# Dilated attention: eight equal steps a pass in place of four pairs

## The chip, the cores and the metric

One core of a Trainium2 chip runs the whole program. The metric is the device time of one execution in microseconds (us), median of several runs. The engines are TensorE (PE, whose weight loads are listed apart as PEld), VectorE (DVE), ScalarE (ACT), GpSimd (POOL) and SyncE (SP). They run their own instruction streams and meet by semaphores.

## What is computed

Two transformer-like blocks on one sequence of 1024 rows by 1024 features, all in float32. The change touches one stage of the second block, attention in three dilations:

```python
DILATED_GROUPS = ((128, 1), (512, 4), (2048, 16))
for g, (window, dilation) in enumerate(DILATED_GROUPS):
    q = partial_rope(qkv[:, :, 0, g], positions)
    k = partial_rope(qkv[:, :, 1, g], positions)
    o, lse = dilated_attention(q, k, qkv[:, :, 2, g], window, dilation)
    outs.append(o)
    lses.append(lse)
alpha = jax.nn.softmax(jnp.stack(lses, axis=0), axis=0)
attn = jnp.sum(alpha[..., None].astype(x.dtype) * jnp.stack(outs, axis=0), axis=0)
```

Inside a dilation the rows are split into residue classes, and each block of 128 queries sees its own and the previous 128 keys of its class (band mask, softmax, product with the values). There are 8 heads of 64. `qkv` is a product of the normed input with columns of `w_in`. A later stage (spatial gating) needs other columns of the same product.

## The kernel before

**Passes.** The stage `Dilated` works in 12 passes. Pass `i` is one pair of heads in one of the dilations (1, 4 and 8 in turn, the last standing for 16 with a mask). A pass has 8 blocks `b` of 128 queries. While a pass does its attention, TensorE fills in the projection of later passes: four feature tiles of queries and keys for pass i+1 and two of values for pass i+2, each of 24 matmuls of 512 columns (line 319, called feature passes below; 8 of high halves first, then 16 with low halves), so 144 feature passes in a pass. In pass 11 and the end of pass 10 nothing is left to project, and 16 gate tiles (line 274, 24 matmuls of 256 columns each) for the stage behind stand there.

**A block** on TensorE is a turn (line 2896: 2 or 4 transposes of the probabilities `PB` into bank 6), the values (line 2908: 2 or 4 program instructions, twice as many rows in the trace, into bank 7) and the scores of the block two further on (line 2879: 2 program instructions, 4 in the trace, of 128 or 256 columns). Blocks with a previous block of their class have the larger form. Between them: DVE adds the mask and takes the row maximum (`top`, line 2778), ACT takes the exponentials (`exps`, line 2651) and copies the turned probabilities out of bank 6 (`take_turned`, line 2661), DVE copies the output rows out of bank 7 (`rows`, line 2785), and POOL stores them (line 2714).

**Around it.** DVE rotates each query or key tile: `rotate` (lines 2747 and 2749) reads the bank, `rotate_end` (lines 2757 and 2761) writes `QR` or `KR`. A bank that held tile n is free for tile n+2 when tile n is rotated, so `qk` and `v` wait for `rotated`; gate tiles 0 and 1 wait for the last two rotations. `turn_v` (line 2861, 4 transposes, two of them a pass) turns the values of the next pass into bank 6, ACT copies them out (`v_rows`, line 2638). One pass in three from pass 5 has `turn_pair` twice (line 2542, 4 transposes of the combined rows into bank 6, copied out by `pair_features`, line 2548). Each weight unit is loaded by SP, split by ACT into a high half (`split_hi`, line 258) and by POOL into a low half (`split_lo`, line 266).

**Order.** It is written out by hand for each engine. A pass is four quarters of two blocks. TensorE does in each: half a tile (12 feature passes), turn b, scores b+2, half a tile, values b, turn b+1, half a tile, values b+1, scores b+3, and behind them a `turn_v` (quarters 0 and 1) or a `turn_pair` (quarters 2 and 3). ACT, DVE and POOL follow the same quarters. On POOL the split of a unit stands behind the store of block 0:

```python
                    store(i, 0)
                    if i + 2 < self.N:
                        split_lo(e, self.v_unit(i + 2), KT * P)
                    else:
                        split_lo(e, unit_no(self.u + 2 * self.N + i - 10))
```

Of the kernel before, what the change touches and what calls it, by code (L numbers as in the profile page):

```python
# [86 lines left out]
def hybrid_kernel(nc, A, out):  # L87
    ctx = ExitStack()
    with ctx:
# [217 lines left out]
        def tile_part(pe, u, m, half, bank, n, ready, begins, part):  # L307
# [4 lines left out]
            lo, hi = {None: (0, 24), 0: (0, 12), 1: (12, 24)}[part]  # L312
# [2108 lines left out]
        class Dilated(Stage):  # L2421
# [44 lines left out]
            def gate_tile(self, i, j):  # L2466

                return 12 * (i - 10) + j - 8 if i == 11 or (i == 10 and j >= 8) else -1
# [140 lines left out]
            def act(self, e):  # L2609
# [7 lines left out]
                def gate_tile(i, j):  # L2617
                    s = self.gate_tile(i, j)
                    if s >= 0:
# [54 lines left out]
                for i in range(self.N):  # L2674
                    qk, v = i + 1 < self.N, i + 2 < self.N
                    for q in range(4):
                        b = 2 * q
                        if q == 3 and v:
                            features(i + 2, 0)
                        gate_tile(i, 3 * q)  # L2680
                        take_turned(i, b)
                        exps(i, b + 2)
                        if q == 3 and self.pair_at(i, 0) is not None:

                            self.load_pair(e, self.pair_at(i, 0))
                        if q == 2 and self.pair_at(i, 1) is not None:
                            self.pair_exps(e, self.pair_at(i, 1))
                        gate_tile(i, 3 * q + 1)
                        take_turned(i, b + 1)
                        gate_tile(i, 3 * q + 2)  # L2690
                        exps(i, b + 3)
                        if q == 0:
# [4 lines left out]
                        if q == 2 and v:  # L2697
                            split_qk(i + 2)
                        if q == 2 and not qk:
                            split_hi(e, unit_no(self.u + 2 * self.N + 2))  # L2700
                        if q < 2 and qk:
                            v_rows(i + 1, q)
                        if q >= 2 and self.pair_at(i, 2) is not None:
                            self.pair_features(e, self.pair_at(i, 2), q - 2, 6)
                        if q == 3 and v:
# [31 lines left out]
            def dve(self, e):  # L2737
# [55 lines left out]
                for i in range(self.N):  # L2793
                    more = i + 1 < self.N
                    for q in range(4):
                        b = 2 * q
                        if q == 1 and more:
                            rotate(i + 1, 1)
                        top(i, b + 2)
                        if q == 1 and more:  # L2800
                            rotate_end(i + 1, 1)
                        if q % 2 == 0 and more:
                            rotate(i + 1, (0, 0, 3)[q])
                        rows(i, b)
                        if q % 2 == 0 and more:
                            rotate_end(i + 1, (0, 0, 3)[q])
                        if q == 1 and more:
                            rotate(i + 1, 2)
                        rows(i, b + 1)
                        top(i, b + 3)  # L2810
                        if q == 1 and more:
                            rotate_end(i + 1, 2)
                        c = self.pair_at(i, 1)
                        if c is not None and q == 1:
                            self.pair_largest(e, c)
                        if c is not None and q == 2:
                            self.pair_shares(e, c)
                            self.pair_weighted(e, c, 0)
                        if c is not None and q == 3:
                            self.pair_second(e, c)  # L2820
                        if q == 0 and self.pair_at(i, 2) is not None:
                            self.pair_third(e, self.pair_at(i, 2))

            def pe(self, e):

                def qk(i, n, part):
                    if part == 0:
# [7 lines left out]
                def v(i, n, part):  # L2835

                    if part == 0:
# [16 lines left out]
                def turn_v(i, n):  # L2854
                    e.wait_ge(v_feat.sem, self.vf + 2 * i + 2)
                    if i:

                        e.wait_ge(p_taken.sem, self.pt + 8 * (i - 1) + 2 * n + 2)
# [23 lines left out]
                def turn_p(i, b):  # L2882
# [3 lines left out]
                    if b in (2, 4) and i + 1 < self.N:  # L2886
# [326 lines left out]
```

## Time and profile before

| | us |
|---|---|
| median of 3 runs (3544.68 to 3549.17) | 3545.74 |
| the profiled execution, its own time | 3545.94 |
| its span in the trace | 3544.1 |
| PE busy, share of the span | 3467.8, 98% |
| the 12 passes, first scores to last values | 1823.0 to 2400.0 |

A row of a timeline gives the start, the duration and the instruction, with `x4` where equal neighbours are merged, and in brackets the engine's idle time before it and who ended it. The ends of matmuls are modelled and overlap the next one, so what a matmul costs on TensorE is read from start to start and not from its duration. The granted clock is given as a share of 2.4 GHz.

### The profile page before, as it was taken

The numbers are of one execution on the slowest core, as the hardware profiler recorded it, in microseconds if no ns is written. First come the engines' busy times: TensorE is split into PE (matmuls) and PEld (weight loads), VectorE is DVE, ScalarE is ACT, GpSimd is POOL, SyncE is SP. The second block draws the span as 40 slices with busy tenths as digits, with TensorE's granted clock in tenths as the row PEclk, the third lists the DMA queues.
The fourth block names the chain that finished last, engine by engine and source line by source line (L and its number), as shares of the span: only waits on it lengthen the run. The fifth ranks groups of instructions, "written<-read, shape, count | busy, mean of one in ns | idle before, by whom it ended". The sixth has DMA issues, their size and how long they took to land.

```text
span 3544.1 us, 44150 instructions
## 1 busy us (share of the span) xinstructions
PE 3467.8 (98%) x17275; PEld 2866.0 (81%) x17275; DVE 1393.4 (39%) x2446; ACT 931.5 (26%) x1568; POOL 959.9 (27%) x415
## 2 busy tenths in 40 slices
PE   7899999999999999999999999999999999999999
PEld 6688877888888888888778878887888888888887
DVE  6873443122445333333653344435123322231224
ACT  4233434222242111111433333333222311111112
POOL 1352102232315333333212222212322232322321
PEclk9999999999999999999999999999999999999999
DMA  4233012212212111111221212213122111111111
GB/s 132 56 80 90 31 54 66 66 48 76 95 65 102 47 47 48 52 53 47 72 87 48 66 47 66 77 36 129 55 71 101 48 54 48 47 47 47 47 47 60
DMA packets 203979, 226.85 MB, mean 64 GB/s; under 512 B 19225, under 2 KB 177605, under 8 KB 203341
## 3 DMA queue, kind: packets, MB, share of 16 engines
q1 hardware_dynamic: 180524, 171.16, 15.8%
q10 hardware_dynamic: 18944, 43.22, 3.5%
q0 software_dynamic: 4384, 10.74, 0.9%
q8 instruction: 85, 1.39, 0.2%
q14 instruction: 42, 0.34, 0.0%
HBM read 191.30 MB, written 31.69 MB: 63 GB/s over the span
## 4 chain that ended last, share of the span: by engine, by line
PE 90%; DVE 5%; ACT 2%; issue 1%; DMA 1%; POOL 0%; SPq 0%; ACTq 0%; DVEq 0%; POOLq 0%
PE ps L274 18%; PE ps L319 16%; PE ps L295 13%; PE ps L302 13%; PE ps L301 13%; PE ps L778 5%; PE ps L2908 2%; PE ps L2879 1%; PE ps L336 1%; PE ps L2391 1%; PE ps L2896 1%; PE ps L510 1%; PE ps L2372 1%; POOL wlo L266 0%; DVE tm L1615 0%
## 5 line engine op out<-in xcount | busy, mean ns | idle before, releaser
L266 POOL TENSOR_TENSOR wlo<-raw,whi 128x2048 fp32r<-128x2048 f32 (+1 forms) x162 | 700.1, 4322 | 1695.4 <-ACT whi L258 1694.7
L301 PE MATMUL ps<-h_lo,whi 128*128 128x512 f32 x1856 | 722.0, 389 | 0.0
L302 PE MATMUL ps<-h_hi,wlo 128*128 128x512 f32 x1856 | 722.0, 389 | 0.0
L258 ACT ACTIVATE whi<-raw 128x2048 fp32r<-128x2048 f32 (+1 forms) x162 | 288.1, 1778 | 903.0 <-PE ps L295 599.2
L295 PE MATMUL ps<-h_hi,whi 128*128 128x512 f32 x1856 | 459.2, 389 | 2.7 <-issue 2.7
L295 PEld LDWEIGHTS ps<-h_hi,whi 128*128 128x128 f32 x1856 | 347.8, 188 | 75.8 <-issue 3.8
L301 PEld LDWEIGHTS ps<-h_lo,whi 128*128 128x128 f32 x1856 | 348.4, 188 | 72.5
L302 PEld LDWEIGHTS ps<-h_hi,wlo 128*128 128x128 f32 x1856 | 348.3, 188 | 72.3
L1198 DVE TENSOR_TENSOR big<-big,ps 128x512 f32<-128x512 f32 x400 | 274.7, 687 | 241.8 <-PE ps L274 241.5
L319 PE MATMUL ps<-h_lo,whi 128*128 128x512 f32 x880 | 351.5, 399 | 0.1
L319 PE MATMUL ps<-h_hi,wlo 128*128 128x512 f32 x880 | 344.3, 391 | 0.0
L274 PE MATMUL ps<-whi,f_hi 128*128 128x512 f32 x800 | 311.2, 389 | 0.0
L274 PE MATMUL ps<-wlo,f_hi 128*128 128x512 f32 x800 | 311.2, 389 | 0.0
L274 PE MATMUL ps<-whi,f_lo 128*128 128x512 f32 x800 | 311.2, 389 | 0.0
L319 PE MATMUL ps<-h_hi,whi 128*128 128x512 f32 x880 | 230.4, 404 | 6.9 <-DVE cacc L1842 6.6
L1132 POOL TENSOR_TENSOR f_lo<-fv,f_hi 128x512 fp32r<-128x512 f32 x108 | 142.2, 1317 | 316.6 <-DVE f_hi L1189 316.6
L319 PEld LDWEIGHTS ps<-h_lo,whi 128*128 128x128 f32 x880 | 165.2, 188 | 40.9 <-issue 5.7
L319 PEld LDWEIGHTS ps<-h_hi,whi 128*128 128x128 f32 x880 | 159.6, 190 | 45.4 <-DVE cacc L1842 7.0
L319 PEld LDWEIGHTS ps<-h_hi,wlo 128*128 128x128 f32 x880 | 165.4, 188 | 32.6
L1183 DVE TENSOR_TENSOR fv<-fr,ps 128x512 f32<-128x512 f32 x44 | 30.2, 687 | 404.8 <-PE ps L302 404.8
L1072 ACT ACTIVATE fr<-ps 128x512 f32<-128x512 f32 x108 | 64.2, 598 | 447.0 <-PE ps L302 445.3
L274 PEld LDWEIGHTS ps<-whi,f_lo 128*128 128x128 f32 x800 | 150.2, 188 | 31.2
(335 smaller groups left out, 4796.3 us busy)
## 6 DMA issues: line engine op xcount, KB each, us to landing
raw<-in_w_ff_dram SPq DMA_DIRECT2D x32, 1024.0 KB, 5.2
raw<-in_w_in_dram SPq DMA_DIRECT2D x57, 512.0 KB, 4.5
raw<-in_w_in_dram SPq DMA_DIRECT2D x28, 1024.0 KB, 5.4
raw<-in_w_ffn_gate_dram SPq DMA_DIRECT2D x11, 1024.0 KB, 5.4
raw<-in_w_ffn_up_dram SPq DMA_DIRECT2D x11, 1024.0 KB, 5.4
raw<-in_w_ffn_down_dram SPq DMA_DIRECT2D x11, 1024.0 KB, 4.9
yt<-y_keep ACTq DMA_DIRECT2D x16, 512.0 KB, 4.0
raw<-in_w_out_dram SPq DMA_DIRECT2D x8, 1024.0 KB, 5.1
```

The lines of the kernel that those rows point to most:

```text
L258: nc.scalar.activation(whi[c % 2][:, 0:cols], raw[c % 2][:, 0:cols], ACT.Copy).then_inc(s_hi.sem, 1)
L266: nc.gpsimd.tensor_tensor(wlo[c % 2][:, 0:cols], raw[c % 2][:, 0:cols], whi[c % 2][:, 0:cols].bitcast(F32), ALU.subtract).then_inc(s_lo.se ...
L274: last = nc.tensor.matmul(out_, lhs(a, k), rhs(b, k), start=(k == 0 and n == 0), stop=(k == ks - 1 and n == 2))
L295: first = nc.tensor.matmul(ps[:, bank + n, :], w(0, k, m * P, P), src[0][:, k, sl], start=k == 0, stop=False)
L301: nc.tensor.matmul(ps[:, bank + n, :], w(0, k, m * P, P), src[1][:, k, sl], start=False, stop=False)
L302: last = nc.tensor.matmul(ps[:, bank + n, :], w(1, k, m * P, P), src[0][:, k, sl], start=False, stop=k == ks - 1)
L319: x = nc.tensor.matmul(ps[:, bank, :], w(a, k, m * P, P), H[b][:, k, sl], start=j == 0, stop=j == 23)
L778: return nc.tensor.matmul(ps[:, t, :], H[a][:, 4 * (j % 2) + k, t * P:(t + 1) * P], w[j](b, k, 0, HALF), start=start, stop=stop)
L1072: nc.scalar.activation(fr[:, n, :], ps[:, n, :], ACT.Relu if self.g == 1 else ACT.Silu).then_inc(act_a.sem, 1)
L1132: nc.gpsimd.tensor_tensor(f_lo[:, c % 2, m, half * HALF:(half + 1) * HALF], fv[:, n % 2, :], f_hi[:, c % 2, m, half * HALF:(half + 1) * HA ...
L1198: nc.vector.tensor_tensor(dst, dst, ps[:, 4 + t % 4, :], ALU.add).then_inc(dve_b.sem, 1)
L2908: last = nc.tensor.matmul(ps[:, 7, h * HD:(h + 1) * HD], PT2[:, b % 2, h, c, :], V2[:, i % 2, b - 1 + c, h, :], start=c == cs[0], stop=c == 1)
```

## The change

A pass becomes eight equal steps, one for each block. TensorE does in step b: 9 feature passes, what stands between (a `turn_v` in steps 1 and 2, a `turn_pair` in steps 6 and 7), 9 feature passes, turn b, values b-1, scores b+2. A tile is cut wherever a step ends. The values come one step later than their turn, also over the pass's end, and so do `rows` on DVE and the stores on POOL. DVE's rotations stand in steps 1, 2, 3 and 5: `rotate`, then `rows` of the block before, `top`, then `rotate_end`. On ACT `split_hi` of the value unit (or of a gate unit) moves from behind `exps` of block 3 to behind that of block 2, and that of the next query and key unit from the end of the third quarter to the end of step 5. No instruction is added or taken out.

```diff
-                    for q in range(4):
-                        b = 2 * q
-                        half_tile(3 * q)
+                    for b in range(8):
+                        tiles = list(self.gate_tiles(i, b))
+                        passes(18 * b, 18 * b + 9)
+                        for t in tiles[1:]:
+                            gate_tile(t - 1)
+                        between(b)
+                        passes(18 * b + 9, 18 * b + 18)
+                        for t in tiles[-1:]:
+                            gate_tile(t)
                         turn_p(i, b)
+                        if 8 * i + b:
+                            value(*divmod(8 * i + b - 1, 8))
                         score(i, b + 2)
...
+            def gate_tiles(i, b):
+
+                if i == 10:
+                    return {5: (0,), 6: (1,), 7: (2, 3)}.get(b, ())
+                if i == 11:
+                    return range(4 + b // 2 * 3 + b % 2 * 2, 6 + b // 2 * 3 + b % 2)
+                return ()
...
+                    for b in range(8):
+                        n = {1: 0, 2: 1, 3: 2, 5: 3}.get(b) if i + 1 < self.N else None
+                        if n is not None:
+                            rotate(i + 1, n)
+                        if 8 * i + b:
+                            rows(*divmod(8 * i + b - 1, 8))
                         top(i, b + 2)
+                        if n is not None:
+                            rotate_end(i + 1, n)
```

TensorE before, two blocks in the middle of a pass of dilation 8 (`PB` is turned, `PT` the turned probabilities, `KR,QR` the scores):

```order
L2896 MATMUL ps<-cst,PB 128x128 x2
L2879 MATMUL ps<-KR,QR 128x128 x2
L319 MATMUL ps<-h_lo,whi 128x512
...
L2908 MATMUL ps<-V,PT 128x64 x2
L2896 MATMUL ps<-cst,PB 128x128 x2
L319 MATMUL ps<-h_hi,whi 128x512 x8
...
L2908 MATMUL ps<-V,PT 128x64 x2
L2879 MATMUL ps<-KR,QR 128x128 x2
L2861 MATMUL ps<-cst,VF 128x128 x4
```

TensorE of the change, the same place:

```order
L319 MATMUL ps<-h_hi,whi 128x512 x3
L2851 MATMUL ps<-cst,VF 128x128 x4
L319 MATMUL ps<-h_hi,whi 128x512 x5
...
L2884 MATMUL ps<-cst,PB 128x128 x2
L2896 MATMUL ps<-V,PT 128x64 x2
L2869 MATMUL ps<-KR,QR 128x128 x2
L319 MATMUL ps<-h_lo,whi 128x512
```

Three places a pair where feature passes break off have become one a block; no values stand behind a feature pass any more, and each `turn_v` stands between two runs of them.

TensorE of the change in pass 10, steps 5 and 6, with gate tiles 0 and 1 (`ps<-whi,h_hi` to `ps<-whi,h_lo` is one tile):

```order
L319 MATMUL ps<-h_hi,wlo 128x512
L274 MATMUL ps<-whi,h_hi 128x256
...
L274 MATMUL ps<-whi,h_lo 128x256
L2884 MATMUL ps<-cst,PB 128x128 x4
L2896 MATMUL ps<-V,PT 128x64 x2
L2869 MATMUL ps<-KR,QR 128x256 x2
L274 MATMUL ps<-whi,h_hi 128x256
```

DVE of the change at that place, the last rotation of all:

```order
L2746 STREAM_SHUFFLE rp<-ps 128x512
L2748 SCALAR_TENSOR_TENSOR rt<-ps,rope 128x512
L2784 COPY OS<-ps 128x2x64
L2777 ISA PB,OS<-ps,mask_p 128x256
L2777 ISA OS 128x1
L2777 ISA PB,OS<-ps,mask_p 128x256
L2777 ISA OS 128x1
L2756 SCALAR_TENSOR_TENSOR rp<-rp,rope 128x512
L2760 TENSOR_TENSOR KR<-rt,rp 128x8x64
```

Before, `top` of block 7 stood behind the end of this rotation; now it stands ahead of it, and TensorE has nothing between the scores of block 7 and gate tile 1, which waits for the rotation.

## Rows read from the trace of the kernel before

**Rows 1.** The page, part 1: busy time, share of the span, instructions.

```profile
PE 3467.8 (98%) x17275; PEld 2866.0 (81%) x17275; DVE 1393.4 (39%) x2446; ACT 931.5 (26%) x1568; POOL 959.9 (27%) x415
```

**Rows 2.** Waits of PE, 1820 to 2402 us: total, times, longest.

```profile
PE ps L274 <- POOL wlo L266: 4.1, 1, 4.1
PE ps L2896 <- ACT YC L2548: 1.2, 3, 0.4
PE ps L2896 <- ACT V L2638: 0.8, 1, 0.8
```

**Rows 3.** Timeline of PE in pass 4 (dilation 4), one pair of blocks.

```profile
2018.10 0.39 PE L319 MATMUL ps<-h_lo,whi 128*128 128x512 f32 x1
...
2018.78 0.39 PE L319 MATMUL ps<-h_hi,wlo 128*128 128x512 f32 x1
2019.01 0.38 PE L2896 MATMUL ps<-cst,PB 128*128 128x128 f32 x2
2019.32 0.49 PE L2879 MATMUL ps<-KR,QR 64*128 64x128 f32 x4
2019.75 0.50 PE L319 MATMUL ps<-h_lo,whi 128*128 128x512 f32 x1
2020.08 0.39 PE L319 MATMUL ps<-h_hi,wlo 128*128 128x512 f32 x1
...
2022.61 0.56 PE L2908 MATMUL ps<-V,PT 128*128 128x64 f32 x4
2023.00 0.60 PE L2896 MATMUL ps<-cst,PB 128*128 128x128 f32 x4
2023.36 2.10 PE L319 MATMUL ps<-h_hi,whi 128*128 128x512 f32 x8
...
2026.22 1.00 PE L2908 MATMUL ps<-V,PT 128*128 128x64 f32 x8
2027.15 0.70 PE L2879 MATMUL ps<-KR,QR 64*128 64x256 f32 x4
2027.78 0.65 PE L2861 MATMUL ps<-cst,VF 128*128 128x128 f32 x4
2028.19 0.47 PE L319 MATMUL ps<-h_lo,whi 128*128 128x512 f32 x1
2028.51 0.39 PE L319 MATMUL ps<-h_hi,wlo 128*128 128x512 f32 x1
```

**Rows 4.** Timeline of PE in pass 11: gate tiles, an ordinary one and the late one.

```profile
2341.82 0.38 PE L274 MATMUL ps<-whi,h_hi 128*128 128x256 f32 x1
...
2344.79 0.55 PE L2908 MATMUL ps<-V,PT 128*128 128x64 f32 x4
...
2364.21 0.49 PE L2879 MATMUL ps<-KR,QR 64*128 64x128 f32 x4
2368.79 0.58 PE L274 MATMUL ps<-whi,h_hi 128*128 128x256 f32 x1 [4.09 <-POOL wlo L266]
...
2373.82 0.55 PE L2908 MATMUL ps<-V,PT 128*128 128x64 f32 x4
```

**Rows 5.** Stretches: length, busy us of PE, PEld, DVE, ACT, POOL, granted clock, DMA.

```profile
1752.00:1755.00 3.00, 3.00 (x13) 2.61 (x12) 2.93 (x4) 0.65 (x1) 0.00 (x0) 0.54 0.00 0
...
2368.00:2370.00 2.00, 1.21 (x5) 1.21 (x6) 0.00 (x0) 0.00 (x0) 1.25 (x2) 0.50 0.05 10
```

**Rows 6.** Timeline of PE in an earlier stage, around another wait.

```profile
1751.73 1.50 PE L510 MATMUL ps<-cst,xn 128*128 128x128 f32 x8 [2.67 <-DVE xn L491]
```

**Rows 7.** Timelines of PE and DVE, pass 4: scores, a rotation's last step.

```profile
2039.30 0.70 PE L2879 MATMUL ps<-KR,QR 64*128 64x256 f32 x4
...
2041.55 1.21 DVE L2761 TENSOR_TENSOR KR<-rt,rp 128x512 f32<-128x512 f32 x1
```

**Rows 8.** Timeline of POOL, pass 11: a store of rows, and the late low half.

```profile
2345.96 0.54 POOL L2714 DMA_DIRECT2D dil_keep<-OS  x1 [7.25 <-DVE OS L2785]
...
2364.24 4.50 POOL L266 TENSOR_TENSOR wlo<-raw,whi 128x2048 fp32r<-128x2048 f32 x1 [6.00 <-ACT whi L258]
```

More of the change, by code:

```diff
@@ L2464, in take_pairs @@
                 return pair_loaded.take(48 * n), pair_step.take(13 * n), pair_exp.take(n), ct_turned.take(2 * n), ct_taken.take(2 * n)
-            def gate_tile(self, i, j):
-                return 12 * (i - 10) + j - 8 if i == 11 or (i == 10 and j >= 8) else -1
+            @staticmethod
+            def gate_tiles(i, b):
[4 more added lines that the diff above has]
+                return ()
             @staticmethod
@@ L2923, in pe, with passes @@
                 for i in range(self.N):
-                    def half_tile(j):
-                        n, part = j // 2, j % 2
-                        if n < 4 and i + 1 < self.N:
-                            qk(i + 1, n, part)
-                        elif n >= 4 and i + 2 < self.N:
-                            v(i + 2, n - 4, part)
-                        elif self.gate_tile(i, j) >= 0:
-                            gate_tile(self.gate_tile(i, j))
-                    for q in range(4):
-                        b = 2 * q
-                        half_tile(3 * q)
+                    def passes(lo, hi):
+                        for n in range(lo // 24, 6):
+                            part = max(lo - 24 * n, 0), min(hi - 24 * n, 24)
+                            if part[0] >= part[1]:
+                                break
+                            if n < 4 and i + 1 < self.N:
+                                qk(i + 1, n, part)
+                            elif n >= 4 and i + 2 < self.N:
+                                v(i + 2, n - 4, part)
@@ new lines, in between @@
+                    def between(b):
+                        if b in (1, 2) and i + 1 < self.N:
+                            turn_v(i + 1, b - 1)
+                        if b in (6, 7) and self.pair_at(i, 2) is not None:
+                            e.wait_ge(p_taken.sem, self.pt + 8 * i + b)
+                            self.turn_pair(e, self.pair_at(i, 2), b - 6, 6)
+                    for b in range(8):
+                        tiles = list(self.gate_tiles(i, b))
[6 more added lines that the diff above has]
+                            gate_tile(t)
@@ L2936, in pe @@
                         turn_p(i, b)
+                        if 8 * i + b:
+                            value(*divmod(8 * i + b - 1, 8))
                         score(i, b + 2)
-                        half_tile(3 * q + 1)
-                        value(i, b)
-                        turn_p(i, b + 1)
-                        half_tile(3 * q + 2)
-                        value(i, b + 1)
-                        score(i, b + 3)
-                        if q < 2 and i + 1 < self.N:
-                            turn_v(i + 1, q)
@@ L2946, in pe @@
-                        if q >= 2 and self.pair_at(i, 2) is not None:
-                            e.wait_ge(p_taken.sem, self.pt + 8 * i + b + 2)
-                            self.turn_pair(e, self.pair_at(i, 2), q - 2, 6)
+                value(self.N - 1, 7)
         class SpatialGate(Stage):
```

78 lines of the change are left out of this document (27 added, 51 removed).

## The prediction

> **What bounds the kernel now.** I read the page's busy times first: PE is busy for 98% of the span and nobody else for more than 39% [rows 1]. A busy PE may still lose time, since the ends of its matmuls are modelled, so I read the waits of PE in the stage, and then its timeline from start to start. The waits are few: one of 4.1 us for a late low half of a weight unit, three of 1.2 us together for ACT's copy of combined rows, one of 0.8 us for ACT's copy of values [rows 2]. An idle time counts from the end of the last matmul, which is 0.39 us long, where the next usually starts 0.23 us after its start; each wait thus costs 0.16 us more than the view shows: 1.7 us for the three and 0.95 us for the one. All else in the stage's 577 us is instructions at their own pace. So the stage is bound by TensorE's starts, and the change can give or take at three places: the pace where one kind of matmul follows another, the waits that go, and the waits that come.
>
> **The pace at the joints.** A feature pass follows another by 0.68 / 3 = 0.23 us [rows 3]. From the last feature pass of a run to the second of the next run, less two such starts, is what a joint costs. In one pair of blocks of pass 4 [rows 3]:
> - turn (2), scores (128 columns): 2018.78 to 2020.08 is 1.30 us, less 0.46: 0.84.
> - values (4), turn (4): 0.23 to the first, then 0.39, then 0.36, and 0.31 to the second feature pass (the x8 has its second 0.31 in, by the 0.32 of 2028.19 to 2028.51 after transposes of the same kind). 1.29 less 0.46: 0.83.
> - values (8), scores (256), without the `turn_v`: 0.23, 0.93, 0.63, and 0.33 to the second feature pass behind scores (2019.75 to 2020.08). 2.12 less 0.46: 1.66.
>
> Sum 3.33 us a pair. Inside these: a value matmul costs 0.11 (8 against 4 of them differ by 0.54 less the 0.10 by which scores start later behind values than a turn does), but the first behind a feature pass only 0.06 (4 take 0.39, and 4 x 0.11 is 0.44). A transpose costs 0.11, and 0.20 where scores follow it. In the change each block is turn, values, scores between two runs:
> - small turn, large values, scores (128): 0.23 + 0.22 + 0.98 + 0.43 + 0.33 = 2.19, less 0.46: 1.73.
> - large turn, small values, scores (256): 0.23 + 0.44 + 0.54 + 0.63 + 0.33 = 2.17, less 0.46: 1.71.
>
> Sum 3.44, so 0.10 to 0.11 us more a pair. Two things make it: both values of a pair lose the cheap start behind a feature pass (2 x 0.05), and the breaks of the runs, fewer as they are (two in place of three), now all end in the dear return from scores. Over 47 pairs I take 0.10 each: **4.7 us**. The passes of the other dilations have the same joints in other sizes, and the difference is in the joints. The gate tiles break off in the same way.
>
> A `turn_v` stood behind scores and took the dear return on itself: it added 0.41 us from its first transpose to the feature pass (2027.78 to 2028.19) and made the return 0.32 instead of 0.33, so 0.40 us. Between two runs it costs 0.23 + 3 x 0.11 + 0.03 + 0.31 less 0.46, 0.44 us. 22 of them at 0.04 make **0.9 us**. Pace in all: +5.6 us. No row shows values directly behind a turn. The bounds are the cheap start kept (95 x 0.05 us less, so +0.8) and a start as late as that of scores behind a turn (0.09 more for 95, so +14). I take the 0.11 since values and transposes follow each other at 0.11 in the other order (4 values, 0.39 us to the turn), and one kind of fp32 matmul of 128 columns of weights to the next costs that in every row but the two with scores, which use half the rows of the array.
>
> Behind scores the second feature pass starts 0.33 us after the first in place of 0.23, and four values behind a feature pass save 0.05 [rows 3]: at one joint the next weights come late, at the other they come in under the long matmul ahead. The Trainium skill, "TensorE: Matmul & The Clock Gate", section "What happens when you issue a matmul", says that TensorE's queue pulls weight loads ahead of matmuls in flight. If that held at each joint, none would cost anything, before or after, and the sum would be without the 5.6 us; the 0.33 speaks against it, the 0.05 for it.
>
> **Waits that go.** The turn waited three times for the copy of combined rows and once for that of values, because the copies out of bank 6 came late on a busy ACT. In the change nine feature passes stand behind each of them (9 x 0.23 = 2.1 us), ACT has had step b's `exps` by then and copies in 0.6 us. On ACT `split_hi` of 1.9 us stands ahead of the first `pair_features`; it begins some 2.3 us after step 5's scores and ends 4.2 us after them, the copy at 4.8, and the turn that needs it starts 5.3 us after them. So I let these waits go: **-2.65 us**. If the cover is gone they cost what they cost now.
>
> **The late low half.** Gate tile 8 waits for POOL's low half. Before, ACT's `split_hi` behind `exps` of block 3 decided. Now that is a block earlier, and POOL's own queue decides: `store(11, 0)` stands ahead and waits for the rows of block 0, which come a step later. From the values of a block to the store's start 1.17 us pass [rows 4, 8], then 0.54 for its issue and 4.50 for the low half [rows 8]: 6.2 us after the values of block 0. TensorE gets from those values to gate tile 8 by 0.54 (small values to scores), 0.43 (scores) and one gate tile of 2.97 us [rows 4]: 3.9 us. So a wait of 2.3 to 2.5 us stands where 4.58 less 0.43, 4.15 us, stood [rows 4]: **-1.75 us**.
>
> **A new wait.** Gate tile 1 in pass 10 waits for the last rotation. Before, half a tile of other work and two blocks' turns lay between. Now `rotate_end` stands behind `top` of block 7, `top` behind the scores of block 7, and those behind gate tile 0; and TensorE comes from these scores directly to gate tile 1. With scores of 256 columns the last step of a rotation that follows `top` ends at 2041.55 + 1.21 = 2042.76, which is 3.46 us after the scores' start at 2039.30 [rows 7]. TensorE would start the tile 0.63 us after it [rows 3]. **+2.9 us.**
>
> **The end of the stage.** The values of blocks 6 and 7 now follow with nothing between, and the second waits for DVE's copy of the first out of bank 7; the last `turn_pair` also stands right behind a block. From values to the store 1.17 us pass, of which the copy's end is some 0.85 us in, and four values cover 0.44. I take **+0.8 us** for both; 0 if something covers them, 1.5 if both wait for the whole way.
>
> **The clock.** The granted clock fell to 1.2 GHz (0.50) in the late wait of 4.09 us [rows 5], and the gate tile behind it took 2368.79 to 2373.82, 5.03 us, against 2.97 us for an ordinary one [rows 4]: 2.06 us. It also fell after an idle time of 2.67 us in an earlier stage (0.54 granted behind it) [rows 5, 6]. So each of the two waits of 2.9 and 2.4 us may bring it down, or not. I take that one of them does, at 2.0 us, as now: **0**. The bounds are none (-2.0) and both (+2.1).
>
> **Sum.** +5.6 - 2.65 - 1.75 + 2.9 + 0.8 + 0 = +4.9 us. Against the profiled execution's 3545.94 (span 3544.1, 1.8 around it, and 0.2 above the median) that is 3550.8 us. The stage behind starts its own chain with the last rows, so that it moves with them.
>
> **Rivals.**
> - *The joints cost nothing more.* If values behind a turn start as cheaply as behind a feature pass, the pace is +0.8 and the time 3546.1. For it: four values behind a feature pass do save 0.05. Against: the saving needs a long matmul ahead, under which the next weights come in, and a turn's are short. Chance 8%.
> - *The rotation is late in every pass* (slower). Tile 2 starts 12 feature passes into step 2 and needs the rotation that ends in step 1 or so; tile 5 the same in steps 5 and 6. Those twelve end 0.63 + 0.33 + 10 x 0.23 = 3.3 us, and the thirteenth would start 3.5 us, after the scores; the rotation ends after 3.46. There is no slack where scores have 256 columns. It decides from a chain longer than 3.5 us. With 0.3 us more on DVE, 20 such starts cost 6 us: 3556.8. Against: the 3.46 us are measured with both `top`s in them, tile 2 also has a `turn_v` of 0.4 us ahead, and the last step is 0.5 us shorter where the dilation is 1. Chance 12%.
> - *Both new waits bring the clock down* at 2.06 us each: 3552.9, just at the bound of 0.2%. Chance 22%, half of it beyond the bound with the spread of the other terms.
> - *Faster by over 0.2%.* It needs stalls in the old order that starts don't show, or both waits gone and the joints free. Chance 3%.
>
> **How the numbers follow.** A measurement of this kernel can tell about 0.2%, 7.1 us, from no change. The forecast has 55%, with its own range of 3548.5 to 3552.5. Within 0.2% are the forecast, the free joints and half of the case with the clock twice down: 55 + 8 + 11 = 74%. Slower are the late rotations and the other half, 12 + 11 = 23%. Faster 3%. The range of 3546 to 3555.5 takes in the free joints, and both falls of the clock with 2.5 us for the end and the joints; it leaves out most of the late rotations and the gain.
>
> **What would show it.** Right: behind a turn the first values start 0.11 us later, a pair of blocks costs 3.44 us over its feature passes; PE's waits are one of about 2.5 us idle on `rotated` near 2342 us and one of 2.0 us on the low half near 2370; the waits for ACT's copies are gone; a pass is 0.4 to 0.5 us longer. Wrong: waits of feature passes on DVE in each pass, or a pass that is not longer. The forecast falls if the gate tile's wait is covered, or if the clock behaves otherwise than once down.

## The result, and the profile after

| | before | after |
|---|---|---|
| median of four runs, us | 3546.44 (3544.68 to 3549.17) | 3569.75 (3568.49 to 3571.7) |
| ratio, 95% interval | 1 | 1.0064 (1.0049 to 1.0079) |
| profiled execution, us (span) | 3545.94 (3544.1) | 3571.7 (3569.9) |
| stage, first scores to last values, us | 1822.97 to 2400.03: 577.1 | 1825.86 to 2424.69: 598.8 |

The change makes the kernel 23.3 us slower. The forecast was 4.9 us slower, and 3569.75 lies far outside the range of 3546 to 3555.5. Of the 25.8 us between the two spans 21.8 are in the stage. 2.9 lie ahead of it, where the kernel is the same: the first 80 us took 1.1 us more in this execution, the clock fell once more near 150 us (2.6 us) and once less near 1770 us (0.9 us back). 1.1 lie behind the stage.

The page of the changed kernel shows at once that nothing new is bound by throughput. Its first part, which answers [rows 1]:

```profile
PE 3477.1 (97%) x17275; PEld 2871.6 (80%) x17275; DVE 1430.0 (40%) x2446; ACT 935.9 (26%) x1568; POOL 958.6 (27%) x415
```

PE gained 9 us of busy time, and 16 us of idle time came in. DVE grew by 37 us with the same 2446 instructions, and that is the odd number of this page. The waits of PE in the stage (engine, line, waited for: total, times, longest; one more of 0.2 us is in both kernels) answer [rows 2]:

```profile
PE ps L319 <- DVE QR L2760: 15.5, 11, 3.4
PE ps L274 <- DVE KR L2760: 2.7, 1, 2.7
PE ps L274 <- POOL wlo L266: 2.3, 1, 2.3
PE ps L2896 <- DVE OS L2784: 0.5, 1, 0.5
PE ps L2869 <- ACT V L2642: 0.4, 1, 0.4
```

The waits for ACT's copies out of bank 6 are gone, the one for the gate tile and the one for the low half are there, and on top stand eleven waits of feature passes for a rotation, one in each of passes 0 to 10. The prediction had named just this view as the sign that it is wrong. From start to start, the late passes cost 1.2 to 1.5 us each in passes 0 to 9 and 3.6 us in pass 10: 17.4 us.

In pass 4 the timelines of PE, DVE and POOL (start, duration, idle time before, releaser) read:

```profile
2038.99 0.40 PE L319 MATMUL ps<-h_lo,whi 128*128 128x512 f32 x1
2039.22 0.40 PE L319 MATMUL ps<-h_hi,wlo 128*128 128x512 f32 x1
2040.89 1.43 PE L319 MATMUL ps<-h_hi,whi 128*128 128x512 f32 x5 [1.27 <-DVE QR L2760]
```

```profile
2036.35 0.42 DVE L2777 CUSTOM_DVE_ANT_0 PB<-ps,mask_p 128x256 f32<-128x256 f32 x1 [0.44 <-PE ps L2869]
2036.70 0.08 DVE L2777 DVE_READ_ACCUMULATOR2_ANT OS<- 128x1 f32 x1
2036.70 0.42 DVE L2777 CUSTOM_DVE_ANT_0 PB<-ps,mask_p 128x256 f32<-128x256 f32 x1
2037.05 0.08 DVE L2777 DVE_READ_ACCUMULATOR2_ANT OS<- 128x1 f32 x1
2037.05 2.68 DVE L2756 SCALAR_TENSOR_TENSOR rp<-rp,rope 128x512 f32<-128x512 f32 x1
2039.76 1.08 DVE L2760 TENSOR_TENSOR QR<-rt,rp 128x512 f32<-128x512 f32 x1
```

```profile
2036.20 0.54 POOL L2713 DMA_DIRECT2D dil_keep<-OS  x1 [5.51 <-DVE OS L2784]
2036.76 2.41 POOL L266 TENSOR_TENSOR wlo<-raw,whi 128x1024 fp32r<-128x1024 f32 x1
```

One instruction is far too long here: the first step of `rotate_end` takes 2.68 us, where 33 others in the stage take 0.69. It ends at 2039.73, 0.56 us after POOL's subtraction, which runs from 2036.76 to 2039.17. Its two inputs, `rp` and the table `rope`, are both in SBUF, as are POOL's `raw` and `whi`. The two instructions of `top` beside it, which take one input from PSUM, keep their 0.42 us under the same subtraction. In pass 10 the low half is that of a gate unit and takes 4.58 us, and there the step takes 4.84:

```profile
2330.59 4.84 DVE L2756 SCALAR_TENSOR_TENSOR rp<-rp,rope 128x512 f32<-128x512 f32 x1
```

```profile
2330.30 4.58 POOL L266 TENSOR_TENSOR wlo<-raw,whi 128x2048 fp32r<-128x2048 f32 x1
```

Of the 37 us that DVE grew by, 23 are these steps' (25.6 in eleven long ones, less 2.8 in three of the kernel before). Another 13 are three instructions that combine the dilations' rows, with both inputs in SBUF too: two of 128x48 take 4.48 and 4.51 us in place of 0.21, and one of 128x1024 takes 5.84 in place of 1.22, each beside a low half of 4.56. The first, on DVE and then POOL:

```profile
2065.16 4.48 DVE L2520 TENSOR_TENSOR cw<-cw 128x48 f32<-128x48 f32 x1
```

```profile
2065.01 4.56 POOL L266 TENSOR_TENSOR wlo<-raw,whi 128x2048 fp32r<-128x2048 f32 x1 [3.07 <-ACT whi L258]
```

No wait of PE hangs on these three.

What brings the step and the subtraction together is POOL's queue. `split_lo` stands behind `store(i, 0)` in both kernels. Before, the rows of block 0 came in its own step, and the split behind the store still waited 5.4 us for ACT's high half. Now that half is ready some 4 us ahead of the store, the rows come a step later, `rows(i, 0)` stands on DVE just ahead of `top` and `rotate_end`, and the store and the split start behind it, 0.3 us ahead of `rotate_end` (in three passes 0.2 us behind its start).

The kernel before had shown the same thing once, in rows that I did not read. In pass 10 its rotation's step took 3.20 us, under a low half of 4.58:

```profile
2318.60 3.20 DVE L2757 SCALAR_TENSOR_TENSOR rp<-rp,rope 128x512 f32<-128x512 f32 x1
```

```profile
2316.66 4.58 POOL L266 TENSOR_TENSOR wlo<-raw,whi 128x2048 fp32r<-128x2048 f32 x1 [6.30 <-ACT whi L258]
```

It cost nothing there, since no matmul was waiting for that rotation. Two other steps of 0.81 us began 0.26 us before a subtraction ended. And those two subtractions show the reverse: VectorE's addition for the combined rows (128x1024, two inputs in SBUF) ran its usual 1.23 us from 2075.95, and POOL's, which began 0.56 us behind it, took 2.91 us in place of 2.4 (the same at 2218.58 and 2219.14):

```profile
2076.51 2.91 POOL L266 TENSOR_TENSOR wlo<-raw,whi 128x1024 fp32r<-128x1024 f32 x1 [4.21 <-ACT whi L258]
```

The rest of the stage's 21.8 us: the waits that were forecast, their falls of the clock, and the pace. The gate tile and the low half (PE, a gate tile's first matmul behind scores of 256 columns in pass 10, and one behind another gate tile in pass 11):

```profile
2359.70 0.70 PE L2869 MATMUL ps<-KR,QR 64*128 64x256 f32 x4
2363.09 0.39 PE L274 MATMUL ps<-whi,h_hi 128*128 128x256 f32 x1 [2.69 <-DVE KR L2760]
...
2389.19 0.28 PE L274 MATMUL ps<-whi,h_lo 128*128 128x256 f32 x1
2391.78 0.39 PE L274 MATMUL ps<-whi,h_hi 128*128 128x256 f32 x1 [2.31 <-POOL wlo L266]
```

And the stretches at the lower clock (length, busy us of PE, PEld, DVE, ACT, POOL, granted clock, DMA):

```profile
2337.87:2344.70 6.83, 6.83 (x24) 5.57 (x23) 2.63 (x8) 1.26 (x5) 0.56 (x1) 0.50 0.26 87
...
2392.49:2395.90 3.41, 3.41 (x19) 3.41 (x18) 1.55 (x2) 0.00 (x0) 0.00 (x0) 0.50 0.90 294
```

By start-to-start times the stage of before is 568.2 us of pace, 6.8 of waits and 2.1 of the lower clock. The stage of after is 570.8 of pace, 23.6 of waits (17.4 for the rotation, 2.8 for the gate tile, 2.5 for the low half, 0.6 and 0.3 at the end) and 4.5 of the clock. The differences, 2.6 + 16.8 + 2.4, make the 21.8.

### The profile page after: what moved, and what is told of

Read it like the earlier page. It is cut to its first block, busy times and chain, and to the rows that moved or that the text cites. A ratio compares the mean times of both kernels' runs of the same rounds, so it can differ in the third digit from the quotient of the medians.

```text
span 3569.9 us, 44150 instructions
## 1 busy us (share of the span) xinstructions
PE 3477.1 (97%) x17275; PEld 2871.6 (80%) x17275; DVE 1430.0 (40%) x2446; ACT 935.9 (26%) x1568; POOL 958.6 (27%) x415
## 4 chain that ended last, share of the span: by engine, by line
PE 89%; DVE 6%; issue 1%; ACT 1%; DMA 1%; POOL 1%; ACTq 0%; SPq 0%; DVEq 0%; POOLq 0%
PE ps L274 18%; PE ps L319 16%; PE ps L295 13%; PE ps L302 13%; PE ps L301 13%; PE ps L778 5%; PE ps L2896 2%; PE ps L2869 1%; PE ps L336 1%; PE ps L2391 1%; DVE rp L2756 1%; PE ps L2884 1%; PE ps L2372 1%; PE ps L510 1%; POOL wlo L266 0%
## 5 line engine op out<-in xcount | busy, mean ns | idle before, releaser
L295 PE MATMUL ps<-h_hi,whi 128*128 128x512 f32 x1856 | 459.2, 389 | 2.7 <-issue 2.7
L319 PE MATMUL ps<-h_hi,whi 128*128 128x512 f32 x880 | 239.6, 409 | 22.3 <-DVE QR L2760 15.5
L274 PEld LDWEIGHTS ps<-whi,f_hi 128*128 128x128 f32 x800 | 150.2, 188 | 31.2
```

Of the source, the lines that this page charges most:

```text
L274: last = nc.tensor.matmul(out_, lhs(a, k), rhs(b, k), start=(k == 0 and n == 0), stop=(k == ks - 1 and n == 2))
L295: first = nc.tensor.matmul(ps[:, bank + n, :], w(0, k, m * P, P), src[0][:, k, sl], start=k == 0, stop=False)
L319: x = nc.tensor.matmul(ps[:, bank, :], w(a, k, m * P, P), H[b][:, k, sl], start=j == 0, stop=j == 23)
```

## The experiments

Theory A: VectorE's step with two inputs in SBUF is kept out while GpSimd subtracts. Its rival B: the rotation is too slow for its twelve feature passes whatever GpSimd does, as the second rival of the prediction had it. Medians are compared with the kernel before on the same chip, 3545.7 to 3547.1 us.

**The split ahead of the store** takes away what makes them meet, and no work.

```
                 for i in range(self.N):
-                    store(i, 0)
                     if i + 2 < self.N:
                         split_lo(e, self.v_unit(i + 2), KT * P)
...
-                    for b in range(1, 5):
+                    for b in range(5):
                         store(i, b)
```

> The changed kernel with one edit: GpSimd's `split_lo` stands ahead of `store(i, 0)`, not behind it. It then waits only for ScalarE's `split_hi`, which in pass 4 ends at 2032.3 us, and would run from there to about 2034.7 us, clear of the rotation's `rp` step at 2037.05 us. Theory A (the `rp` step is held for as long as GpSimd's subtraction runs): `rp` takes 0.69 us in every pass instead of 2.7 to 3.2 (4.84 in pass 10), the eleven waits of feature tile 2 for rotation 0 go (17.4 us), and with the one of pass 10 its fall of the clock (2.4 us). The low half of the gate units comes earlier too, since its store no longer stands ahead (2.5 us, and perhaps the clock's 2.1). From 3569.8 that gives 3545.5 to 3550 us. Theory B (the chain of the rotation is too long for the twelve feature passes whatever GpSimd does): the chain and its waits of 1.2 to 1.4 us a pass stay, 3562 to 3568 us.

Measured: 3546.38 us, a ratio of 0.9999 (0.9989 to 1.0009) to the kernel before. The eleven waits are gone. DVE and then POOL in pass 4:

```profile
2029.58 0.69 DVE L2755 SCALAR_TENSOR_TENSOR rp<-rp,rope 128x512 f32<-128x512 f32 x1
2030.30 1.13 DVE L2759 TENSOR_TENSOR QR<-rt,rp 128x512 f32<-128x512 f32 x1
```

```profile
2024.88 2.41 POOL L266 TENSOR_TENSOR wlo<-raw,whi 128x1024 fp32r<-128x1024 f32 x1 [1.65 <-ACT whi L258]
```

The rotation ends at 2031.43 and tile 2 starts at 2031.99 as the passes ahead of it set it, so 0.56 us are to spare. That accounts for the wait: the step ended 2.68 - 0.69 = 1.99 us late, less the 0.56 to spare, 1.43 us, where 1.44 were measured. B falls. One step, in pass 10, still meets the end of a low half of 4.58 us and takes 1.38; no matmul waits for it. The stage takes 577.2 us, 21.6 less than after: 17.4 of these waits, 1.6 of the low half (0.9 us late in place of 2.5), some 2 of the clock, 0.3 at the end.

**Moving the collision.** Here the split stands one step later, where it meets rotation 1.

```
                     store(i, 0)
+                    if i < 11:
+                        store(i, 1)
                     if i + 2 < self.N:
                         split_lo(e, self.v_unit(i + 2), KT * P)
```

> The changed kernel with one edit: in passes 0 to 10 `split_lo` stands behind `store(i, 1)`, one step later (pass 11 as it was). In pass 4 it would start at about 2042.8 us, just as the `rp` step of rotation 1 does. Theory A: the collision moves, it does not go: `rp` of rotation 0 takes 0.69 us, `rp` of rotation 1 takes 2.3 to 3.2 us in each pass (4.5 to 4.9 in pass 10). Nobody waits for it, since tile 3 starts only in step 4, so the eleven waits of feature passes go (17.4 us) with the clock's fall behind that of pass 10 (2.4 us); the wait of the low half in pass 11 stays: 3549 to 3552 us. Theory B: the long step belongs to rotation 0 and its place, so it stays there: 3568 to 3571 us.

Measured: 3549.65 us, ratio 1.0009 (1.0000 to 1.0019). All eleven long steps are still there, 2.69 to 3.20 us and 5.35 in pass 10, but on rotation 1, whose tile starts in step 4. In pass 4 (DVE, then POOL):

```profile
2033.10 3.16 DVE L2758 SCALAR_TENSOR_TENSOR rp<-rp,rope 128x512 f32<-128x512 f32 x1
```

```profile
2033.29 2.41 POOL L266 TENSOR_TENSOR wlo<-raw,whi 128x1024 fp32r<-128x1024 f32 x1
```

The eleven steps take even more DVE time than in the changed kernel (35.1 us against 33.1), and TensorE waits once, 1.3 us in pass 10, a wait that I had not expected. So the price of the collision is set by who needs the result. It also shows that the long step goes with POOL's instruction, not with its own place.

**Cutting the subtraction.** Two kernels test what "kept out" means: four pieces that follow each other directly (for every unit of 1024 columns, two earlier stages included), and four with a moment between them (value units of this stage alone).

```
+            step = 256 if cols == KT * P else cols
+            for lo in range(0, cols, step):
+                last = nc.gpsimd.tensor_tensor(wlo[c % 2][:, lo:lo + step], raw[c % 2][:, lo:lo + step],
+                                               whi[c % 2][:, lo:lo + step].bitcast(F32), ALU.subtract)
+            last.then_inc(s_lo.sem, 1)
```

> The changed kernel with one edit: the low half of a unit of 1024 columns is made in four subtractions of 256 columns, one after another at the same place in GpSimd's queue (the units of 2048 columns stay whole). GpSimd is as busy as before, and at the same time. Theory A in its strict form (the VectorE instruction is held to the end of the one GpSimd instruction that is running): `rp` is held for at most one piece of about 0.6 to 0.7 us, its time falls from 2.7 to 3.2 us to at most 1.4, and the waits of passes 0 to 9 (13.8 us) shrink to 0 to 0.3 us each; 3554 to 3560 us, the wait of pass 10 stays at 3.6. Theory C (VectorE gets a smaller share of something for as long as GpSimd works, whatever the length of its instructions): `rp` still ends with the last piece, or is slowed in proportion, and the waits stay at 1.2 to 1.4 us each; 3568 to 3571 us.

Measured: 3572.46 us, ratio 1.0074 (1.0057 to 1.0091). POOL's four pieces take 2.83 us where the whole took 2.41, and the step is held over all four:

```profile
2036.07 3.09 DVE L2759 SCALAR_TENSOR_TENSOR rp<-rp,rope 128x512 f32<-128x512 f32 x1
```

```profile
2035.78 2.83 POOL L268 TENSOR_TENSOR wlo<-raw,whi 128x256 fp32r<-128x256 f32 x4
```

The strict form of A falls, and C stands so far, though its 3568 to 3571 us had left out that four pieces take longer than one. The waits grew by what POOL's work grew: 0.42 us each, from 1.44 to 1.85, and the stage by 3.9 us.

```
+                        for x in range(4):
+                            if x:
+                                last.then_inc(piece.sem, 1)
+                                e.wait_ge(piece.sem, 3 * i + x)
+                            last = nc.gpsimd.tensor_tensor(...)
```

> The changed kernel with one edit: in passes 0 to 9 the low half of the value unit is made in four subtractions of 256 columns as before this, but GpSimd waits for the end of each before it issues the next, so that it stands still for a moment between them. Theory A2 (VectorE's instruction is let in as soon as GpSimd has none running, and not while the next follows directly): the `rp` step waits for one piece at most; 0.69 to 1.4 us in place of 3.1, QR earlier by some 1.5 us, the waits of passes 0 to 9 gone or below 0.3 us; with that of pass 10 (3.6 us) left, 3553 to 3558 us. Theory C (VectorE is kept out, or slowed, until GpSimd's work of the unit is done): `rp` lasts 3 us or more and the waits stay at 1.4 to 1.9 us: 3569 to 3575 us.

Measured: 3558.62 us, ratio 1.0035 (1.0021 to 1.0050). Now the two engines take turns. In pass 4 (DVE, then POOL):

```profile
2028.30 1.03 DVE L2766 SCALAR_TENSOR_TENSOR rp<-rp,rope 128x512 f32<-128x512 f32 x1
2029.36 1.64 DVE L2770 TENSOR_TENSOR QR<-rt,rp 128x512 f32<-128x512 f32 x1
```

```profile
2028.02 4.41 POOL L2729 TENSOR_TENSOR wlo<-raw,whi 128x256 fp32r<-128x256 f32 x4
...
2030.00 1.61 POOL L2729 TENSOR_TENSOR wlo<-raw,whi 128x256 fp32r<-128x256 f32 x1
```

The step and the addition each wait for a piece, and the pieces wait in their turn: one of them (the second POOL row, the third of the four) lasts 1.61 us, one that meets nobody takes 0.74, and the four take 4.41, of which the three pauses are 0.23. The waits of passes 0 to 9 fall to 0.35 us in three passes and to none in the others. This trace is of an execution of 3552.92 us, the fastest of the five, and the median is 0.6 us above A2's range; but the stage in it is 12.1 us shorter than in the changed kernel, and the medians, each less that of the kernel before on its chip, are 11.8 apart. C falls, and A2 holds: a lock that is handed over when its holder has nothing that follows directly, not a share.

**Which inputs.** The step takes its first input from PSUM, the unshuffled tile, so that this kernel doesn't compute the rotation and only its times are of use.

```
-                    nc.vector.scalar_tensor_tensor(out=rp[:, :], in0=rp[:, :], scalar=(-0.125, 1.0)[k],
+                    nc.vector.scalar_tensor_tensor(out=rp[:, :], in0=ps[:, n % 2 if i else n, :], scalar=(-0.125, 1.0)[k],
```

> The changed kernel with one edit: the `rp` step of `rotate_end` takes its first input from PSUM (the tile as it stands, not its shuffled copy, so that the rotation's values are others); the second is still the table in SBUF. Same engine, place and size. Theory D (only a VectorE instruction with both inputs in SBUF is kept out while GpSimd subtracts): `rp` takes about 0.7 us in the midst of GpSimd's subtraction, and the addition behind it (QR, both inputs in SBUF) is held instead, from about 2037.7 to 2039.2 plus its own time, 2.4 to 2.6 us in place of 1.1; QR ends some 0.5 us earlier, the waits of passes 0 to 9 shrink from 1.4 to about 0.8 us: 3561 to 3566 us. Theory E (any VectorE instruction that touches SBUF is kept out): `rp` takes 2.7 us as before, 3568 to 3571 us.

Measured: 3558.07 us, ratio 1.0030 (1.0019 to 1.0042). D is right and E falls. In pass 4 the step runs its 0.69 us in the midst of the subtraction, and the addition is held in its place:

```profile
2031.18 0.69 DVE L2756 SCALAR_TENSOR_TENSOR rp<-ps,rope 128x512 f32<-128x512 f32 x1
2031.90 2.43 DVE L2760 TENSOR_TENSOR QR<-rt,rp 128x512 f32<-128x512 f32 x1
```

```profile
2030.89 2.43 POOL L266 TENSOR_TENSOR wlo<-raw,whi 128x1024 fp32r<-128x1024 f32 x1
```

The time is 3 us under what I expected, which had counted on 0.8 us for each wait. They are 0.5 to 0.8, and 2.9 in place of 3.6 in pass 10, and the clock fell once in the stage (0.50 granted from 2348.5 to 2355.3 us), not twice.

**The rotation's end ahead of `top`.** POOL's queue is left as it is.

```
+                        if n is not None:
+                            rotate_end(i + 1, n)
                         top(i, b + 2)
-                        if n is not None:
-                            rotate_end(i + 1, n)
```

> The changed kernel with one edit on VectorE: in the steps with a rotation `rotate_end` stands ahead of `top`, directly behind `rows`; GpSimd's queue is as in the changed kernel. In pass 4 the `rp` step would run from 2035.8 to 2036.5 us, ahead of GpSimd's subtraction, and the addition behind it (both inputs in SBUF) would start at 2036.54, some 0.2 us before the subtraction at 2036.76. Theory A1 (the one that starts first keeps the other out): the addition takes its 0.7 to 1.2 us, the subtraction's record grows from 2.4 to about 3.3 us, the waits of feature passes go in passes 0 to 9 (13.8 us) and 10, gate tile 1's wait falls from 2.7 to 1.5 us idle: 3547 to 3551 us. Theory A3 (a lead of 0.2 us by the record is none: at 1939.49 us of the changed kernel `rp` began 0.19 us before the subtraction and was held to its end): the addition is held to about 2040.1 us in place of 2040.84, and each of the eleven waits shrinks by some 0.7 us only: 3558 to 3563 us.

Measured: 3562.05 us, ratio 1.0043 (1.0026 to 1.0060). A3 is right, A1 is not. In pass 4 the addition began 0.22 us ahead of the subtraction by their records, and was still held to its end, while the subtraction took its usual time:

```profile
2034.18 0.68 DVE L2756 SCALAR_TENSOR_TENSOR rp<-rp,rope 128x512 f32<-128x512 f32 x1
2034.89 3.62 DVE L2760 TENSOR_TENSOR QR<-rt,rp 128x512 f32<-128x512 f32 x1
```

```profile
2035.11 2.40 POOL L266 TENSOR_TENSOR wlo<-raw,whi 128x1024 fp32r<-128x1024 f32 x1
```

The waits shrink from 1.2 to 1.5 us to 0.5 to 0.8, and `top`, which stands behind the held addition, now comes late for ACT: eight turns wait for its copy of values (3.0 us by the view of waits), a kind of wait that I had not counted.

**Both edits** together, the split ahead of the store and the rotation's end ahead of `top`:

> The changed kernel with two edits: `split_lo` ahead of `store(i, 0)`, and on VectorE `rotate_end` ahead of `top`. Theory A: beside what the first edit brings alone, rotations end 1.5 us earlier and the last one before gate tile 1 asks for it, so that its wait of 2.8 us goes; `top` comes 1.4 to 1.8 us later in four steps of eight, which the 6 us of a step cover. 3542 to 3547 us. Theory B (what `top` loses, the turn of a later step waits for): new waits of TensorE for ScalarE's `PB` of 0.2 to 1 us in four steps of each pass, 3550 to 3580 us.

Measured: 3546.21 us, ratio 0.9998 (0.9988 to 1.0008), at the upper end of A. Of waits like B's one is there, 0.4 us for ACT's copy of values in pass 10, where the step still met a low half and took 2.58 us. The stage takes 574.8 us. Gate tile 1's wait fell only to 1.5 us, because `rotate_end` still stands behind `rows`, which waits for values behind a gate tile. So the last rotation was put ahead of both, on the kernel of the split ahead of the store:

```
+                        if n == 3:
+                            rotate_end(i + 1, n)
                         if 8 * i + b:
                             rows(*divmod(8 * i + b - 1, 8))
                         top(i, b + 2)
-                        if n is not None:
+                        if n is not None and n < 3:
                             rotate_end(i + 1, n)
```

> The kernel of the split ahead of the store (3546.4 us), with one edit on VectorE: in step 5 `rotate_end` stands directly behind `rotate`, ahead of `rows` and `top`, which wait for matmuls behind a gate tile. The last rotation before gate tile 1 then ends near 2336.5 us in place of 2340.2, before TensorE asks for it. Theory A: gate tile 1's wait of 2.7 us goes with the clock's fall of 6.8 us that stands behind it (1.9 to 2.5 us): 3541.5 to 3543.5 us. Theory B (the fall of the clock comes from the small waits around it as well, and only moves): 3543.5 to 3545.5 us.

Measured: 3541.15 us (3538.72 to 3543.4), ratio 0.9986 (0.9977 to 0.9996) to the kernel before: 5.9 us under its 3547.09 on that chip. Its waits of PE in the stage:

```profile
PE ps L274 <- POOL wlo L266: 0.7, 1, 0.7
PE ps L2897 <- DVE OS L2783: 0.5, 1, 0.5
PE ps L2870 <- ACT V L2642: 0.4, 1, 0.4
PE ps L319 <- ACT VF L2637: 0.2, 1, 0.2
```

The gate tile's wait is gone, and the clock stays up through the whole stage, which takes 571.1 us, 6.0 less than before. Theory A is right, with a median 0.35 us below its range: 2.8 of the wait and 2.6 of the clock are 5.4 of the 6.1 us between this stage and that of the first experiment.

**Values behind scores.** The same kernel as in the first experiment, with `score` ahead of `value`, measures the joints that the prediction argued about.

```
                         turn_p(i, b)
+                        score(i, b + 2)
                         if 8 * i + b:
                             value(*divmod(8 * i + b - 1, 8))
-                        score(i, b + 2)
```

> The kernel of the split ahead of the store (3546.4 us), with a block's scores ahead of its values: turn, scores, values. It measures the joints, of which the prediction took 3.44 us a pair. Scores then stand behind a turn, at 0.20 us instead of the 0.54 to 0.98 behind values less their own starts; values stand behind scores, which no row shows, and feature passes behind values, which none shows either. If values pay behind scores what a feature pass pays (0.10 more than behind others) and feature passes start at once behind values, nothing changes but for the gate tile's wait, 0.5 us shorter: 3545 to 3547 us. If the matmuls of half the rows cost at both of their sides, +0.1 us for each of 95 blocks: 3555 us. If the dear return goes, -0.1 us each: 3537 us.

Measured: 3552.52 us, ratio 1.0016 (1.0007 to 1.0026), between two of the three cases. The stage is 5.5 us longer than that of the first experiment; its pace is, by 5.9 us, 0.06 for each of 95 blocks. The dear return did not go with the scores. In the kernel of this experiment a feature pass behind values is followed by the next 0.31 us later:

```profile
2021.97 0.48 PE L319 MATMUL ps<-h_lo,whi 128*128 128x512 f32 x1
2022.28 0.39 PE L319 MATMUL ps<-h_hi,wlo 128*128 128x512 f32 x1
```

That is the return of 0.31 to 0.33 behind turns and scores too [rows 3]. Which of the joints between scores and values costs the 0.06 is left open.

## Why the prediction was wrong

**What bounds the kernel** was right: TensorE's starts, with waits as the only thing that the change could add in size.

**The pace** (forecast +5.6, measured +2.6). Both sizes of step are 0.05 cheaper than summed. Large turn, small values and scores of 256 columns take 2.12 us, from the last feature pass to the second of the next run, where 2.17 was worked out:

```profile
2034.36 0.39 PE L319 MATMUL ps<-h_hi,wlo 128*128 128x512 f32 x1
2034.59 0.60 PE L2884 MATMUL ps<-cst,PB 128*128 128x128 f32 x4
2035.03 0.56 PE L2896 MATMUL ps<-V,PT 128*128 128x64 f32 x4
2035.51 0.70 PE L2869 MATMUL ps<-KR,QR 64*128 64x256 f32 x4
2036.14 0.50 PE L319 MATMUL ps<-h_lo,whi 128*128 128x512 f32 x1
2036.48 0.40 PE L319 MATMUL ps<-h_hi,wlo 128*128 128x512 f32 x1
```

Small turn, large values and scores of 128 take 2.14 for 2.19 (2352.60 to 2354.74 us in pass 10). The term that failed is the cheap start of the first values: to the scores four values behind a turn take 0.48, not the 0.54 of the sum, and eight take 0.93, as they did behind a feature pass [rows 3], not 0.98. So the 0.05 that was written off isn't lost. A pair costs 3.34 us, 0.01 more than before, not 0.11. The `turn_v` costs what was said (2038.09 to 2038.99 in pass 4, 0.90 less 0.46). The rival of the free joints, held at 8%, was right on this term. Pairs and `turn_v` together are some 1.4 us; of the rest about 1 us stands in second passes that are 0.1 us late behind each of the eleven waits.

**The waits that go** (-2.65) and **the late low half** (4.15 to 2.4 forecast, 2.47 measured) were right. **Gate tile 1** was right too: 2.8 us for 2.9. **The end of the stage** was put at 0.8 and measured 0.6 and 0.3.

**The clock** (forecast 0) was half right. It fell twice, not once, 2.4 us more: behind the rotation's wait of 3.4 us in pass 10 and behind the low half's of 2.3. Behind the gate tile's wait of 2.7 us it stayed up in this kernel; in the first experiment, without the rotation's wait ahead, it fell there for 6.8 us. So of the two waits that the prediction had in its sum one brought the clock down, as it said. Which one it would be was not to be had from the profile, and the runs leave it open: where the split paused between four pieces, with the same three waits of 3.4, 2.7 and 2.3 us, the clock fell behind the first (0.51 granted from 2321.2 to 2324.6 us) and the second (0.50 from 2345.1 to 2351.9) and not behind the third.

**The rotation late in every pass** is the step that failed, and it is nearly the whole error. The profiled execution is 20.9 us above the forecast: 17.4 of these waits, 2.4 of the clock, 3.0 less of the pace, and 4.0 outside the stage. The waits and the clock that go with a collision of VectorE and GpSimd stood nowhere in the sum. The prediction had the place. It had said that tile 2 starts twelve feature passes behind the scores, that the chain on DVE takes 3.46 us [rows 7], and from which length it decides. It then took each DVE instruction at a fixed duration. It asked of each queue what is delayed there, and never what runs on POOL beside the step. It had noted that `store(11, 0)` delays the split in pass 11, with the 1.17 us from values to store, and did not carry the same arithmetic to passes 0 to 10, where the same queue puts the split 0.3 us ahead of `rotate_end`. With the duration of 2.7 us that a collision gives, its own sum would have been 1.99 us late, less 0.5 to spare, eleven times, or about 16 us. (The 0.5 is 3.5 less 3.46 and the `turn_v`'s 0.44; the first experiment measured 0.56.) So the rotation was not too slow by itself, as the rival had it: it was held. The rival was priced at 0.3 us more on DVE, 3556.8 us, and given 12%.

The prediction asked what is late next wherever a stall went, but not what comes to run side by side. The evidence was in the trace: one instruction of 44 with 3.20 us instead of 0.69, which a mean of 747 ns over the group hides. It shows one long step under one subtraction; what it takes for the two to exclude each other came only from the experiments. The least and the largest time of a group would have shown it.

The Trainium skill, "SBUF — State Buffer", section "Who interferes with whom", states the rule that was missed: VectorE and GpSimd share a pair of SBUF ports as an exclusive lock, and a VectorE instruction with two SBUF inputs contends with a GpSimd instruction that reads SBUF. By the section "Summary: rules for kernel authors" of the same page the second of these two to issue "fully blocks" until the first finishes. The traces here agree on which instructions contend (0.69 us with one input from PSUM, 2.7 with two from SBUF) and that one is kept out rather than slowed. They differ in two points. GpSimd kept VectorE out over four instructions that followed directly (3.09 us). And VectorE lost with a lead of 0.22 us by the records (3.62 us). Whether a recorded start is the moment of issue no run shows; the order of the recorded starts, at least, does not decide. With a lead of 0.56 us, in the kernel before, VectorE did go first.

## What to carry to other kernels

When a change shifts an engine's queue by a step, list what then runs at the same time on VectorE and GpSimd, and not only who waits for whom: two instructions with no semaphore between them can still exclude each other. Read the largest duration of a group beside its mean; one outlier of 4 times the usual in a group of 44 is a mechanism that a new order may meet every time. The cure was an order and cost nothing: GpSimd's long subtraction goes to a stretch in which VectorE reads from PSUM or stands idle, or at least beside a result that nobody waits for. In these runs the second way was 3.3 us behind the first (3549.65 against 3546.38).

## What the runs showed of the hardware

- A VectorE instruction with both inputs in SBUF (128x512, fp32, 0.69 us) takes 2.67 to 3.16 us when GpSimd's subtraction of 2.41 us runs, and 4.84 under one of 4.58. The subtraction keeps its time in these cases. A multiplication of 128x48, 0.21 us, took 4.48 and 4.51 us in the same way.
- Cutting GpSimd's instruction in four does not help while the pieces follow directly (3.09 us). With a semaphore between them the engines alternate (1.03 and 1.64 us), and GpSimd then pays: 4.41 us in place of 2.83, 0.23 of it for the pauses.
- A lead of 0.22 us by the records did not save VectorE's addition, which took 3.62 us. A lead of 0.56 us did (1.23 us, twice in the kernel before), and GpSimd's subtraction took 2.91 us in place of 2.4.
- VectorE instructions with one input from PSUM were not held: 0.42 us for those of `top`, 0.69 for the step fed from PSUM.
- Eight value matmuls take 0.93 us to the scores behind transposes as they do behind a pass of 512 columns, so their start costs the same behind both.
- Around gate tile 1's wait of 2.7 us TensorE's clock fell to 1.2 GHz for 6.8 us in the first experiment (row below, 0.50 granted). In the changed kernel, where the clock had fallen and risen again after the rotation's wait 26 us earlier, it stayed up at the same wait. That is no rule: with the split in four pieces and pauses the rotation's wait was 24 us earlier, and the clock fell behind both.

```profile
2339.71:2346.54 6.83, 6.23 (x29) 6.23 (x30) 2.74 (x7) 0.66 (x2) 0.00 (x0) 0.50 0.00 0
```
